# A two-layer step of matmul, mLSTM and sparse attention: layer 1 projects the unnormed x and scales the results; operand slices made during the tile before; page numbers read earlier

## The chip, the cores and the metric

The kernel runs on one core of one Trainium2 chip. The metric is device microseconds of one execution, from the first to the last instruction on that core with what the runtime adds around them. The engines are named as in the profile: PE (TensorE matmul), DVE (VectorE), ACT (ScalarE), POOL (GpSimd), SP (SyncE, which here only issues transfers and reads numbers into its registers).

## The reference, cut to what matters

A prompt of 512 tokens and 8 single-token decode samples (520 columns together) go through two layers of width 2048: a pool and mLSTM layer, then a sparse-attention layer with compressed, selected and window branches whose decode samples read a paged cache. Everything is float32.

```python
def rmsnorm(x, g):
    r = lax.rsqrt(jnp.mean(xf * xf, axis=-1, keepdims=True) + EPS)
    return (xf * r).astype(x.dtype) * g

def nsa_layer(x, ..., page_table, norm_g, w_in, b_gate, w_out):
    h = rmsnorm(x, norm_g)
    proj = jnp.einsum('btd,de->bte', h, w_in)
    q, kv_c, kv_s, kv_w, gts, z = split_cols(proj, (NSA_W, KV_W, KV_W, KV_W, 3 * N_HEADS, NSA_W))
    ...
    past_c = cache_kv_cmp[page_table].astype(f32)
    ...
    y = jnp.einsum('bte,ed->btd', o.reshape(B, T, NSA_W).astype(x.dtype) * jax.nn.silu(z), w_out)
    return x + y.astype(x.dtype), kv_c, kv_s, new_win
```

The first layer has the same frame: norm, input projection, mixing, a gate by silu(z), output projection, residual.

## The kernel before, in words

Activations lie transposed, features on the partitions: x is 16 slices of 128 features x 520 columns (`XY`). A projection is a **tile**: 128 output features, its weight 2048 x 128 (1 MB). The program has 146 tiles in a fixed order: one for the gates of layer 0, 16 for the pool part, 40 for the mLSTM (4 heads of 10), 16 for the output of layer 0 (`O0_BASE`), one for the gates of layer 1 (`G1_BASE`), 56 for the attention (`A_BASE`, 4 groups of 14), 16 for the output of layer 1 (`O1_BASE`).

Each float32 product is made of three reduced ones, so both operands are split in a high and a low part. The weight: SP loads `w_raw`, ACT writes its high part `w_hi` (`split_hi`), POOL subtracts and writes `w_lo` in four instructions (`split_lo`). There are two weight buffers: SP may load tile n+2 once POOL has split tile n; ACT splits tile n+2 after it has taken tile n out of PSUM. The activations: `h_hi` by ACT, `h_lo` by DVE, one slice of 16 at a time, made once for a whole stretch of tiles, since PE reads the same 16 slices for each tile. A tile is 96 matmuls (16 slices k, three products, two halves of 260 columns), and waits for the slices two at a time:

```python
for k in range(*part):
    ...
    if h_need is not None and k % 2 == 0:
        pe.wait_ge(S["h_ready"], h_need + k + 2)
```

The 16 slices are rewritten at four places. Before tile 0 and before tile `G1_BASE` they hold the normed x (`h_dve`, `h_act`: DVE multiplies by g and rstd into `x_res`, ACT copies to `h_hi`, DVE subtracts to `h_lo`). Before `O0_BASE` and `O1_BASE` they hold y, the mixed output (`y_split_act`, `y_split_dve`). At each place the rewriting starts when PE has done the last tile that reads the old slices, and PE waits for the first two.

What stands between the layers, in order: the 16 output tiles, during which DVE adds the residual (line 461) and the squares (line 464); the cross-partition sum on PE (`norm_pe`, line 404); rstd by DVE and ACT; the slices; tile `G1_BASE`; a sigmoid and seven small matmuls on the gates; then the first attention tile. In an output tile's turn ACT first squares the row that DVE has taken out (line 473), and only then splits the weight of the tile after next.

SP issues its transfers in one written order, and a wait in it holds all that follow. Before head 0 it issues the eight state loads (line 587), then the weight of the third mLSTM tile. After tile `G1_BASE`'s weights are on their way it saves x to DRAM (line 644) and reads the 32 page numbers into registers (`value_load`, line 650), from which the cache loads of line 670 get their addresses.

In the last part of each mLSTM head DVE updates the decode samples' state (line 1593, 16 instructions) before it normalises the head (lines 1596 to 1601). In an attention group ACT takes all 14 tiles out of PSUM: q, k, v rows with plain copies, the z tiles with a Silu (line 1356).

## Time and profile before

| what | value |
|---|---|
| median of three runs | 2301.4 us (2300.94 to 2303.07) |
| the profiled execution's own time | 2301.22 us |
| its span, first to last instruction | 2299.4 us |
| PE busy | 2165.9 us, 94% |
| DVE, ACT, POOL busy | 831.7, 735.6, 749.2 us |
| mean granted TensorE clock | 0.977 |

The profile lists busy time by engine, the waits between engines, and a timeline in microseconds from the span's start. Neighbouring instructions of one kind are merged in a timeline row, with their count behind an x. In square brackets stands how long the engine was idle before the row, and which instruction released it.

### The profile page before, as it was taken

The numbers are of one execution on the slowest core, as the hardware profiler recorded it, in microseconds if no ns is written. First come the engines' busy times: TensorE is split into PE (matmuls) and PEld (weight loads), VectorE is DVE, ScalarE is ACT, GpSimd is POOL, SyncE is SP. The second block draws the span as 40 slices with busy tenths as digits, with TensorE's granted clock in tenths as the row PEclk, the third lists the DMA queues.
The fourth block names the chain that finished last, engine by engine and source line by source line (L and its number), as shares of the span: only waits on it lengthen the run. The fifth ranks groups of instructions, "written<-read, shape, count | busy, mean of one in ns | idle before, by whom it ended". The sixth has DMA issues, their size and how long they took to land.

```text
span 2299.4 us, 44104 instructions
## 1 busy us (share of the span) xinstructions
PE 2165.9 (94%) x17957; PEld 2049.7 (89%) x17957; DVE 831.7 (36%) x1785; ACT 735.6 (32%) x1029; POOL 749.2 (33%) x588
## 2 busy tenths in 40 slices
PE   3899999999999989978999999999999999999996
PEld 3899999999999989977988998889888998889995
DVE  6412203333150361124246522652255423653114
ACT  4322123323232342223324332442334333343221
POOL 1244433433434234442330242124321233123440
PEclk7999999999999999989999999999999999999997
DMA  6223363746446354453544344343634344414431
GB/s 228 76 79 83 110 199 99 206 129 167 141 112 194 114 129 114 114 176 92 145 113 121 94 126 131 84 129 98 161 92 127 102 135 107 124 53 114 114 102 74
DMA packets 453106, 282.06 MB, mean 123 GB/s; under 512 B 17112, under 2 KB 445720, under 8 KB 450611
## 3 DMA queue, kind: packets, MB, share of 16 engines
q1 hardware_dynamic: 452939, 279.71, 43.5%
q8 instruction: 120, 1.97, 0.4%
q14 instruction: 47, 0.39, 0.1%
HBM read 250.86 MB, written 45.99 MB: 129 GB/s over the span
## 4 chain that ended last, share of the span: by engine, by line
PE 57%; issue 22%; POOL 10%; DVE 8%; ACT 2%; POOLq 0%; DVEq 0%; ACTq 0%
PE ps L365 45%; POOL w_lo L343 10%; PE ps L1028 2%; PE ps L1122 1%; PE ps L933 1%; PE ps L1062 1%; PE ps L1126 1%; PE ps L1100 1%; PE ps L958 1%; DVE scratch L1730 1%; PE ps L1130 1%; ACT scratch L1334 1%; DVE xy L1866 1%; DVE x_res L428 1%; DVE h_lo L425 0%
## 5 line engine op out<-in xcount | busy, mean ns | idle before, releaser
L343 POOL TENSOR_TENSOR w_lo<-w_raw,w_hi 128x512 fp32r<-128x512 f32 x584 | 749.0, 1314 | 1498.4 <-ACT w_hi L327 1167.6
L365 PE MATMUL ps<-h_hi,w_hi 128*128 128x260 f32 x4672 | 975.2, 290 | 58.0 <-DVE h_lo L425 35.4
L365 PE MATMUL ps<-h_hi,w_lo 128*128 128x260 f32 x4672 | 945.7, 284 | 0.0
L365 PE MATMUL ps<-h_lo,w_hi 128*128 128x260 f32 x4672 | 945.0, 284 | 0.0
L365 PEld LDWEIGHTS ps<-h_hi,w_hi 128*128 128x128 f32 x4672 | 728.4, 190 | 90.0 <-issue 62.1
L365 PEld LDWEIGHTS ps<-h_hi,w_lo 128*128 128x128 f32 x4672 | 725.0, 190 | 0.0
L365 PEld LDWEIGHTS ps<-h_lo,w_hi 128*128 128x128 f32 x4672 | 724.9, 190 | 0.0
L327 ACT ACTIVATE w_hi<-w_raw 128x2048 fp32r<-128x2048 f32 x134 | 256.8, 1916 | 27.0 <-DMA w_raw<-in_w_in 18.8
L461 DVE TENSOR_TENSOR xy<-ps,x_res 128x520 f32 x32 | 22.4, 700 | 282.0 <-PE ps L365 282.0
L473 ACT ACTIVATE scratch<-xy 128x520 f32 (+1 forms) x32 | 20.4, 639 | 281.3 <-DVE xy L461 281.3
L1334 ACT ACTIVATE scratch<-ps,scratch 128x128 f32<-128x128 f32 (+3 forms) x128 | 66.3, 523 | 134.1 <-DVE scratch L1758 133.6
L1716 DVE TENSOR_TENSOR scratch<-ps,scratch 128x520 f32<-128x520 f32 x24 | 16.8, 699 | 201.1 <-ACT rstd L1324 201.1
L1212 ACT ACTIVATE scratch<-ps 128x520 f32<-128x520 f32 x24 | 14.5, 604 | 209.2 <-PE ps L365 209.2
L1028 PE MATMUL ps<-scratch 128*128 128x128 f32 (+3 forms) x256 | 80.0, 435 | 0.0
L1509 DVE COPY scratch<-scratch 128x16 f32<-128x16 f32 x4 | 0.7, 184 | 169.7 <-ACT scratch L1212 169.7
L1346 ACT ACTIVATE scratch<-ps 128x128 f32<-128x128 f32 (+1 forms) x64 | 28.0, 437 | 100.0 <-PE ps L1100 99.6
L1028 PEld LDWEIGHTS ps<-scratch 128*128 128x128 f32 x256 | 41.1, 191 | 16.1 <-issue 11.0
L1322 ACT ACTIVATE scratch<-ps 128x520 f32<-128x520 f32 x16 | 9.7, 605 | 139.5 <-PE ps L365 139.5
L1641 DVE COPY scratch<-ps 128x512 f32<-128x512 f32 x32 | 22.1, 692 | 88.2 <-PE ps L933 87.7
L1757 DVE TENSOR_REDUCE scratch<-ps 128x2 f32<-128x256 f32 (+1 forms) x64 | 52.8, 825 | 2.2
L383 ACT ACT_TABLE_LOAD x39 | 50.0, 1283 | 0.9 <-ACT w_hi L327 0.2
L1122 PE MATMUL ps<-scratch 128*128 128x128 f32 x320 | 48.9, 284 | 0.0
(320 smaller groups left out, 1775.0 us busy)
## 6 DMA issues: line engine op xcount, KB each, us to landing
w_raw<-in_w_in SPq DMA_DIRECT2D x114, 1024.0 KB, 5.8
w_raw<-in_w_out SPq DMA_DIRECT2D x32, 1024.0 KB, 6.0
scratch<-in_cache_kv_sel SPq DMA_DIRECT2D x256, 64.0 KB, 1.9
scratch<-in_cache_kv_win SPq DMA_DIRECT2D x128, 128.0 KB, 2.5
scratch<-in_cache_kv_cmp SPq DMA_DIRECT2D x256, 64.0 KB, 2.0
out_kvw_s<-in_cache_kv_win SPq DMA_DIRECT2D x24, 512.0 KB, 6.7
x_scratch<-xy SPq DMA_DIRECT2D x2, 4160.0 KB, 14.3
x_res<-x_scratch SPq DMA_DIRECT2D x32, 260.0 KB, 6.0
```

The lines of the kernel that those rows point to most:

```text
L327: nc.scalar.activation(WH[:, t.p], WR[:, t.p], ACT.Copy).then_inc(S["w_hi"], 1); own.done("w_hi")
L343: ins = nc.gpsimd.tensor_tensor(WL[:, t.p, k:k + 4], WR[:, t.p, k:k + 4], WH[:, t.p, k:k + 4].bitcast(F32), ALU.subtract)
L365: mm = nc.tensor.matmul(PS[:, bank + c, 0:HALF], lhsT=w[:, t.p, k, :], rhs=h[:, k, c * HALF:(c + 1) * HALF], start=(k == 0 and x == 0), st ...
L383: own.step(nc.scalar.activation(CELL[:], ones[0:1, 0:1], func))
L428: nc.vector.scalar_tensor_tensor(XR[:, k % 2], XY[:, k], PR[:, gcol + k:gcol + k + 1], RS[:], ALU.mult, ALU.mult).then_inc(S["h_tmp"], 1); ...
L933: mm = T(PS[:, bank, pg * P:(pg + 1) * P], ring(u)[:, pg], ident)
L958: M(PS[at:at + 32, 6, 0:256], lhsT=zq[:, 32 * b:32 * b + 32], rhs=pt[:, kind, half * 256:(half + 1) * 256], start=(b == 0), stop=(b == NS ...
L1028: mm = M(PS[:, r, 0:(i + 1) * P], lhsT=qt[:, jj, i * P:(i + 1) * P], rhs=kT[:, r, 0:(i + 1) * P], start=True, stop=True)
L1122: M(PS[:, to, 0:P], lhsT=pt[:, 0, s * P:(s + 1) * P], rhs=vr[:, 0, s * P:(s + 1) * P], start=(s == 0), stop=(s == i))
L1334: ins = A(pr[:, 2 * (n % 2) + r, 0:L], PS[:, r, 0:L], ACT.Exp, bias=S1["st"][:, 4 + n % 2, r:r + 1], scale=SCALE, accum_out=S1["st"][:, n ...
L1346: A(pt[:, 0, 0:L], PS[:, 4, 0:L], ACT.Copy).then_inc(S["at_pta"], 1); own.done("at_pta")
L1757: step(V.tensor_reduce(st[:, 2 + n % 2], PS[:, 0:2, 0:(i + 1) * P], AX, ALU.max))
```

## The change

1. Layer 1 no longer norms x before it projects. The slices hold x times g, made by `xg_hi` (ACT) and `xg_lo` (DVE, one instruction with three inputs) slice by slice while PE still runs the last output tile of layer 0; a semaphore `k_read` tells which slices PE has read. rstd lies in a row `r1` of its own, and each result of layer 1 is multiplied by it when it leaves PSUM: the tiles of k and v rows, the z tiles and an extra instruction for q on DVE; cos and sin of the rotation are multiplied by it once. ACT keeps the Silu of z, now from SBUF, and drops its copies.
2. y is split slice by slice in the same way during the last tile before `O0_BASE` (slices 0 to 13) and during the last turns of group 3 before `O1_BASE` (slices 0 to 6).
3. In head 3 the 16 state updates stand behind all 16 slices; their eight stores stand in `out_sp` behind its third turn.
4. The page numbers get a buffer of their own, are loaded at the start and read into SP's registers behind the first state loads.
5. `norm_pe` and the small gate matmuls stand inside the tiles `G1_BASE` and `A_BASE`, behind slice 12.
6. One of the six stores of a group's rows is issued three tiles earlier, and the first eight cache units behind the second weight of group 0.

```diff
+                if tell and k < KT - 1:
+                    mm.then_inc(S["k_read"], 1)
...
-            own.step(nc.vector.reciprocal(RS[:], RS[:]))
-
-        def h_dve(dve, own, r, gcol):
+            own.step(nc.vector.reciprocal(RS[:] if out is None else out, RS[:]))
...
+        def xg_hi(act, own, k):
+
+            nc.scalar.activation(HH[:, k], XY[:, k], ACT.Copy, scale=PR[:, R_G1 + k:R_G1 + k + 1]
+                                 ).then_inc(S["h_hi"], 1); own.done("h_hi")
+
+        def xg_lo(dve, own, k):
+            dve.wait_ge(S["h_hi"], KT + k + 1)
+            nc.vector.scalar_tensor_tensor(HL[:, k], XY[:, k], PR[:, R_G1 + k:R_G1 + k + 1], HH[:, k].bitcast(F32),
+                                           ALU.mult, ALU.subtract).then_inc(S["h_ready"], 1); own.done("h_ready")
+
+        def y_hi(act, own, r, ks, done=None):
+
+            for k in ks:
+                if done is None:
+                    act.wait_ge(S["k_read"], (KT - 1) * (2 * r) + k + 1)
+                elif k == ks[0]:
+                    act.wait_ge(S["proj_done"], done)
                 nc.scalar.activation(HH[:, k], XY[:, k], ACT.Copy).then_inc(S["y_hi"], 1); own.done("y_hi")
...
+            empty(7, 0)
+            add_squares(7, 0)
+            for k in range(12 if r == 0 else 0):
+                xg_lo(dve, own, k)
+            empty(7, 1)
+            for k in range(12, 14 if r == 0 else 0):
+                xg_lo(dve, own, k)
+            add_squares(7, 1)
+            for k in range(14, KT if r == 0 else 0):
+                xg_lo(dve, own, k)
...
+            square(7, 0)
+            if r == 0:
+                split_hi(act, own, Tile(base, 0, 7, 2).ahead(2))
+                for k in range(14):
+                    act.wait_ge(S["k_read"], KT - 1 + k + 1)
+                    xg_hi(act, own, k)
+            square(7, 1)
+            if r == 0:
+                for k in range(14, KT):
+                    xg_hi(act, own, k)
+                split_hi(act, own, Tile(base, 1, 7, 2).ahead(2))
...
+            for i in range(8):
+                body(i, i == 7)
+                if i == 2 and late is not None:
+                    late()
...
+            sp.dma_start(PAGES[:], I["page_table"].rearrange("(o b) n -> o (b n)", o=1)).then_inc(S["small_in"], 16)
...
             load_states(0)
+            sp.wait_ge(S["small_in"], 16 * 10)
+            page_of = [sp.value_load(PAGES[0:1, x:x + 1], min_val=0, max_val=I["cache_kv_sel"].shape[0] - 1)
+                       for x in range(NS * NPG)]
...
-            out_sp(sp, 0, O0_BASE, G1_BASE)
+            out_sp(sp, 0, O0_BASE, G1_BASE, lambda: store_states(3))
...
+            project(pe, Tile(G1_BASE, 0), 2 * KT, part=(0, 12))
             norm_pe(pe, 1)
-            project(pe, Tile(G1_BASE, 0), 2 * KT)
-            pe.wait_ge(proj_read[1], (G1_BASE + 1) // 2)
+            project(pe, Tile(G1_BASE, 0), 2 * KT, part=(12, KT))
...
+                    project(pe, Tile(A_BASE, 0, g, 14), part=(0, 12))
+                    gates()
+                    project(pe, Tile(A_BASE, 0, g, 14), part=(12, KT))
...
+                if h == 3:
+                    act.wait_ge(S["m_yz"], 8)
+                    act.wait_ge(S["pl_y"], 9)
+                    y_hi(act, own, 0, range(KT - 2))
...
-                        if r < 4:
-                            A(halves(qr[:, r]), ps2(t), ACT.Copy)
...
+                        z = XR[:, (n // 4) % 2]
+                        A(z, z, ACT.Silu).then_inc(S["a_z"], 1); own.done("a_z")
...
+                    if g == 3 and n >= 12:
+                        y_hi(act, own, 1, ((), range(0, 4), range(4, 7), ())[n - 12])
...
+                if h < 3:
+                    new_states()
...
+                if h == 3:
+                    y_lo(dve, own, 0, range(KT - 2))
...
+                if h == 3:
+                    y_lo(dve, own, 0, range(KT - 2, KT))
+                    new_states()
...
+            TT(cosT, cosT, r1, ALU.mult)
+            step(TT(sinT, sinT, r1, ALU.mult))
...
+                        TT(halves(XR[:, (0, 1, None, 0, None, 1)[x]]), ps2(t), halves(r1), ALU.mult
+                           ).then_inc(proj_read[t.p], 1)
...
+                        if r < 4:
+                            TT(halves(qr[:, r]), ps2(t), halves(r1), ALU.mult)
...
+                            TT(halves(XR[:, jj % 2]), PS[:, 2:4, 0:HALF], halves(r1), ALU.mult).then_inc(proj_read[t.p], 1)
...
+                        y_lo(dve, own, 1, ((), (), range(0, 4), range(4, 7))[n - 12])
```

SP's queue at the start of head 0, before. L587 are the state loads, L303 the weight loads of the third mLSTM tile and on, L598 copies of the window cache:

```order
L587 DMA scratch<-in_state_mlstm_c 128x2x256 x8
L303 DMA w_raw<-in_w_in 128x16x128 [waits w_split]
L598 DMA out_kvw_s<-in_cache_kv_win 16x8192
L303 DMA w_raw<-in_w_in 128x16x128 [waits w_split]
L598 DMA out_kvw_s<-in_cache_kv_win 16x8192
```

The same place in the changed kernel, where L675 is the read of one page number (32 of them) and L304 the weight load:

```order
L625 DMA scratch<-gate_scratch 128x1048 x3
L630 DMA scratch<-in_state_mlstm_c 128x2x256 x8
L675 TENSOR_LOAD pages [waits small_in]
L675 ISA x2
L675 TENSOR_LOAD pages
...
L675 ISA x2
L304 DMA w_raw<-in_w_in 128x16x128 [waits w_split]
L647 DMA out_kvw_s<-in_cache_kv_win 16x8192
L304 DMA w_raw<-in_w_in 128x16x128 [waits w_split]
```

The 32 reads now stand between the state loads and the third tile's weight.

DVE at the end of head 3, before. L1593 is the state update, L1596 to L1608 the norm and gate of the head, L450 the low parts, L461 the first output tile's results:

```order
L1588 TENSOR_TENSOR scratch<-scratch 128x520 [waits m_sq,m_nev]
L1593 SCALAR_TENSOR_TENSOR scratch<-scratch 128x256 [waits v_in,c_sc,m_sqs]
L1593 SCALAR_TENSOR_TENSOR scratch<-scratch 128x256 [waits m_cn] x15
L1596 TENSOR_SCALAR rstd<-ps 128x520 [waits m_ssq,m_cn]
L1598 RECIPROCAL rstd<-rstd 128x520 [waits m_sqrt,m_var]
L1601 SCALAR_TENSOR_TENSOR xy<-xy,params,rstd 128x520 [waits dve_step]
L1601 SCALAR_TENSOR_TENSOR xy<-xy,params,rstd 128x520
L1608 TENSOR_TENSOR xy<-xy,scratch 128x520 [waits proj_read0,dve_step]
L1608 TENSOR_TENSOR xy<-xy,scratch 128x520 [waits m_yz]
L450 TENSOR_TENSOR h_lo<-xy,h_hi 128x520 [waits m_yz,n_out,y_hi,st_out]
L450 TENSOR_TENSOR h_lo<-xy,h_hi 128x520 [waits y_hi,h_ready] x15
L455 MEMSET rstd 128x520 [waits h_ready]
```

And in the changed kernel (L1647 the state update, L464 the low parts, L1666 the gate):

```order
L1652 TENSOR_SCALAR rstd<-ps 128x520 [waits m_ssq,m_sqs]
L1654 RECIPROCAL rstd<-rstd 128x520 [waits m_sqrt,m_var]
L1657 SCALAR_TENSOR_TENSOR xy<-xy,params,rstd 128x520 [waits dve_step]
L1657 SCALAR_TENSOR_TENSOR xy<-xy,params,rstd 128x520
L464 TENSOR_TENSOR h_lo<-xy,h_hi 128x520 [waits y_hi,dve_step]
L464 TENSOR_TENSOR h_lo<-xy,h_hi 128x520 [waits y_hi,h_ready] x13
L1666 TENSOR_TENSOR xy<-xy,scratch 128x520 [waits proj_read0,h_ready]
L1666 TENSOR_TENSOR xy<-xy,scratch 128x520 [waits m_yz]
L464 TENSOR_TENSOR h_lo<-xy,h_hi 128x520 [waits y_hi,m_yz]
L1647 SCALAR_TENSOR_TENSOR scratch<-scratch 128x256 [waits v_in,c_sc,h_ready]
L1647 SCALAR_TENSOR_TENSOR scratch<-scratch 128x256 [waits m_cn] x15
L480 MEMSET rstd 128x520 [waits n_out,st_out,m_cn]
```

The low parts moved ahead of the gate, and the 16 state updates moved from before the norm to just ahead of the output tiles.

ACT from the last output tile of layer 0 on, in the changed kernel (L501 squares, L328 the split of a weight, L444 the slices of x times g, L399 the square root for rstd). Before, the 16 slices stood behind the square root:

```order
L501 ACTIVATE scratch<-xy 128x520 [waits sq_sum,proj_read1]
L328 ACTIVATE w_hi<-w_raw 128x2048 [waits proj_done,w_loaded1,sq_made]
L444 ACTIVATE h_hi<-xy,params 128x520 [waits k_read,w_hi]
L444 ACTIVATE h_hi<-xy,params 128x520 [waits k_read,h_hi] x13
L501 ACTIVATE scratch<-xy 128x520 [waits sq_sum,proj_read0,h_hi]
L444 ACTIVATE h_hi<-xy,params 128x520 [waits sq_made]
L444 ACTIVATE h_hi<-xy,params 128x520 [waits h_hi]
L328 ACTIVATE w_hi<-w_raw 128x2048 [waits proj_done,w_loaded0,h_hi]
L386 ACT_TABLE_LOAD [waits proj_read1,proj_read0]
```

The split of the first attention tile's weight (the second L328) now stands behind all 16 slices.

## Rows read from the trace of the kernel before

**Rows 1.** The page, part 1: engine, busy us, share, instructions.

```profile
PE 2165.9 (94%) x17957; PEld 2049.7 (89%) x17957; DVE 831.7 (36%) x1785; ACT 735.6 (32%) x1029; POOL 749.2 (33%) x588
```

**Rows 2.** Waits of PE by releaser: us in total, times, longest.

```profile
PE ps L365 <- DVE h_lo L425: 35.4, 14, 12.0
...
PE ps L365 <- ACT x_res L1356: 4.2, 12, 0.7
```

**Rows 3.** Timeline of PE: start us, us, what [idle before, releaser].

```profile
306.26 0.80 PE L365 MATMUL ps<-h_hi,w_hi 128*128 128x260 f32 x2 [3.41 <-POOL w_lo L343]
...
831.52 0.77 PE L365 MATMUL ps<-h_hi,w_hi 128*128 128x260 f32 x2 [6.37 <-DVE h_lo L450]
...
1032.04 0.77 PE L365 MATMUL ps<-h_hi,w_hi 128*128 128x260 f32 x2 [10.05 <-DVE h_lo L425]
...
2067.36 0.33 PE L1051 MATMUL ps<-c_common,scratch 128*128 128x128 f32 x1 [1.67 <-DVE scratch L1776]
...
2074.60 0.77 PE L365 MATMUL ps<-h_hi,w_hi 128*128 128x260 f32 x2 [6.91 <-DVE h_lo L450]
```

**Rows 4.** Timeline of SP, ACT and POOL at the first mLSTM tiles.

```profile
289.62 0.63 SPq L303 DMA_DIRECT2D w_raw<-in_w_in  x1
...
299.26 1.92 ACT L327 ACTIVATE w_hi<-w_raw 128x2048 fp32r<-128x2048 f32 x1 [7.21 <-DMA w_raw<-in_w_in]
...
301.25 4.96 POOL L343 TENSOR_TENSOR w_lo<-w_raw,w_hi 128x512 fp32r<-128x512 f32 x4 [19.60 <-ACT w_hi L327]
...
320.91 0.60 ACT L1212 ACTIVATE scratch<-ps 128x520 f32<-128x520 f32 x1 [14.63 <-PE ps L365]
```

**Rows 5.** DMA issues: count, KB each, median us to landing.

```profile
w_raw<-in_w_in SPq DMA_DIRECT2D x114, 1024.0 KB, 5.8
...
scratch<-in_state_mlstm_c SPq DMA_DIRECT2D x8, 256.0 KB, 8.4
...
x_scratch<-xy SPq DMA_DIRECT2D x1, 4160.0 KB, 12.0
```

**Rows 6.** Line 650 alone, two stretches: ns min/median/max, first and last start us.

```profile
L650 SPq TENSOR_LOAD <-scratch x10: 395/860/877, 1019.6 to 1029.6; - x10
...
L650 SPq TENSOR_LOAD <-scratch x23: 263/266/395, 1029.6 to 1042.2; - x23
```

**Rows 7.** Timeline of DVE, ACT and POOL, head 3 to the output tiles.

```profile
822.37 1.43 DVE L1601 SCALAR_TENSOR_TENSOR xy<-xy,params,rstd 128x520 f32<-128x520 f32 x2
...
845.60 0.70 DVE L461 TENSOR_TENSOR xy<-ps,x_res 128x520 f32 x1 [1.35 <-PE ps L365]
...
857.00 0.70 DVE L461 TENSOR_TENSOR xy<-ps,x_res 128x520 f32 x1 [9.12 <-PE ps L365]
...
820.14 0.20 ACT L383 ACTIVATE act_cell<-c_common 1x1 f32<-1x1 f32 x1
...
827.82 10.68 ACT L445 ACTIVATE h_hi<-xy 128x520 fp32r<-128x520 f32 x16
...
827.87 6.35 POOL L343 TENSOR_TENSOR w_lo<-w_raw,w_hi 128x512 fp32r<-128x512 f32 x4 [6.02 <-ACT w_hi L327]
849.33 5.02 POOL L343 TENSOR_TENSOR w_lo<-w_raw,w_hi 128x512 fp32r<-128x512 f32 x4 [15.12 <-ACT w_hi L327]
```

**Rows 8.** Single lines of DVE: ns min/median/max, first and last start.

```profile
L450 DVE TENSOR_TENSOR h_lo<-xy,h_hi x32: 699/700/1671, 828.6 to 2084.0; 128x520 fp32r<-128x520 f32 x32
...
L1593 DVE SCALAR_TENSOR_TENSOR scratch<-scratch x64: 483/485/1398, 402.4 to 816.5; 128x256 f32<-128x256 f32 x64
...
L428 DVE SCALAR_TENSOR_TENSOR x_res<-xy,params,rstd x9: 759/761/1852, 40.9 to 55.3; 128x520 f32<-128x520 f32 x9
```

**Rows 9.** Timeline of DVE and ACT around the tile of the gates.

```profile
1018.46 0.70 DVE L461 TENSOR_TENSOR xy<-ps,x_res 128x520 f32 x1 [9.15 <-PE ps L365]
...
1072.97 0.60 ACT L1322 ACTIVATE scratch<-ps 128x520 f32<-128x520 f32 x1 [14.65 <-PE ps L365]
```

**Rows 10.** Timeline of DVE at the start of the last output tiles.

```profile
2089.26 0.70 DVE L461 TENSOR_TENSOR xy<-ps,x_res 128x520 f32 x1 [3.86 <-PE ps L365]
```

255 lines of the change are left out of this document (130 added, 125 removed).

## The prediction, made blind

> **What bounds the kernel now.** The page's first part comes first: PE is busy 94% of the span [rows 1], so time can only come out of the gaps of PE or out of stretches in which its clock is low. The waits of PE by releaser say who makes the gaps: the low parts that DVE writes for slices of x (35.4 us) are the largest, and ACT's Silu of the z tiles costs 4.2 us in twelve short waits [rows 2]. The timeline of PE says where: 3.41 us ahead of the third mLSTM tile, for a weight; 6.37 us ahead of the output tiles of layer 0; 10.05 us and more at the tile of the gates; 1.67 and 6.91 us ahead of the last output tiles [rows 3]. The first 48 us are not touched by the change, except for one small load more.
>
> A bare tile takes 11.4 us: two successive output tiles are taken out at 845.60 and 857.00 [rows 7]. With it each place has a price, low clock included. From PE's stop at 831.52 - 6.37 = 825.15 to 845.60 are 20.4 us for one tile: 9 us lost. From the last output tile (1018.46) to the first attention tile (1072.97) are 54.5 us [rows 9] for two tiles (22.9) and about 1.8 us for the square sum and the small matmuls: 29.8 us lost. From 2067.4 [rows 3] to 2089.26 [rows 10] are 21.9 us for one tile: 10 us lost. If all of this went and nothing came, 53 us would be gained with the 4.2. I go through the places, because at each one something is put in the way.
>
> **Term 1, page numbers: +16.6.** In front of the third mLSTM tile PE already waits 3.41 us, and the chain behind it is SP's queue: the weight is issued at 289.62, split by ACT from 299.26 (1.92 us), by POOL from 301.25 (4.96 us), and PE starts at 306.26 [rows 3, 4]. The change puts the 32 reads into this queue, ahead of this weight. In the old place they took from 1019.6 to about 1042.7, where they held nothing that PE waited for. The single line shows two speeds: the first ones come 1.11 us apart, the last 22 intervals take 12.6 us, 0.57 us each [rows 6]. The slow ones lie under the save of x, 4.2 MB that land in 12 us [rows 5]. In the new place the state loads are in flight: the last is issued some 2 us before 289.6 and lands 8.4 us later [rows 5], so about four reads are slow and 28 fast: 4.4 + 16.0 = 20.4 us. Then the weight is issued at 310.0, lands 5.8 us later [rows 5] (not 9.6, the state loads are through), ACT 2.0, POOL 5.0: PE starts at 322.9, not 306.26. That is 16.6 us, all on the path: PE has nothing else to do from 302.9 on. All fast would give +14.5, all slow 35.5 us of reads and +31.7. The gap has low clock behind it: the tile begun at 306.26 is taken out at 320.91 [rows 4], 14.65 us where 11.4 and 0.3 would do, so 2.9 us; that is paid before the change too. The next weights are queued behind in the same rhythm and have a tile's time each. In layer 1 nothing is won back, because the cache units that stood behind the reads are needed four tiles later.
>
> **Term 2, the page table's load at the start: +0.4**, one issue more ahead of the small loads; bounds 0 and 1.
>
> **Term 3, output tiles of layer 0: +4.4.** ACT can begin the high parts when its table is in, at 820.4, and needs 10.68/16 = 0.67 us for one [rows 7]; DVE begins the low parts at 823.8, behind the norm, and needs 0.73 us (0.70 [rows 8] and a gap). So PE finds slices 0 and 1 ready at 825.3 and runs on at its own 0.72 us a slice. Two things follow. First, ACT does 14 slices before it takes out the last head tile and splits the next weight: 14 x 0.67 from 820.4, then 0.6 and 1.9 us, end at 832.3, where the split was through at 827.8; POOL's four instructions start at 832.4. While POOL runs, DVE's instruction with both inputs in SBUF does not take 0.70 but up to 1.67 us [rows 8], and POOL's four take 6.35 instead of 5.02 us [rows 7]. The low parts 12 and 13 and the two gate products fall into that: the gate is ready at 839.3, slices 14 and 15 at 840.8 and 841.6. PE waits about 2 us ahead of slice 12 and 4 us ahead of slice 14; the first output tile ends at 843.1, 2 us earlier than before. Second, the 16 state updates now stand ahead of the output tiles: 16 x 0.52 = 8.3 us [rows 8], the zeroing of the row 0.9, so DVE takes the first output tile out at 850.9, not 845.6. Behind that stand ACT's square, the split of the third output tile's weight and POOL: this took from 845.6 to 854.35 [rows 7], 8.8 us. So the third tile can start at 859.7, where it started at 856.7: a loss of 3 us, whatever PE won before it. PE idles 2.5 to 5 us there, and I add 1.4 for a phase of low clock. Bounds: -6 (the updates hide) and +7.
>
> The Trainium skill (SBUF — State Buffer, "Who interferes with whom") says that a VectorE instruction with two SBUF inputs contends with a GpSimd instruction that reads SBUF. The rows agree: 0.70 against 1.67 us. A sum without that rule would have the gate ready 4 us earlier here, and terms 4 and 5 better by 3 us and 2 us.
>
> **Term 4, the gates' tile: -23.5.** Seen from the last output tile's end at 1018.3: ACT squares the row before, splits the weight of the gates' tile until 1010.7, and then makes 14 high parts at 0.67 us, until 1020.1; DVE's instruction of three inputs takes 0.79 us a slice, but up to 1.85 us beside POOL [rows 8], which is busy until 1017.4. So it has slice 3 at 1018.0 and slice 11 at 1024.3, and PE, which needs them from 1018.3 on at 0.72 us, is not held. DVE then takes the last output tile out (1024.3 to 1025.1, 6 us later than before), ACT squares it, makes slices 14 and 15 and only then splits the first attention tile's weight: 1027.2 to 1029.1; POOL until 1034.2. PE is through with the gates' tile and the square sum at 1031.1: it waits 3.2 us, for a weight. Then the first attention tile with its seven small matmuls, 12.7 us, ends at 1047. Before, it ended at 1072.5. That is 25.4 us; a gap of 3.2 us is like that of 3.41 at 306, so I take two thirds of its 2.9 us of low clock off. Bounds: -29 (the weight in time) and -20 (low clock, and the split held up further). The reciprocal and the scaling of cos and sin lie under the first attention tile.
>
> **Term 5, last output tiles: -6.** Low parts 0 to 3 stand in turn 14 ahead of an addition that PE's next transposes wait for; four of them are 2.9 us, of which I count 1.2 as free: PE starts 1.7 us later. The three in turn 15 delay the last combination by 0.75 more. PE then starts the output tile at 2070.2 instead of 2074.6, reaches slice 6 at 2074.5, and waits 1 us for slice 7, because the last gate product runs beside POOL (1.67 us by rows 8) and the low parts follow at 0.73 us. The tile ends at 2082.9, not 2088.9. Bounds -9 and -2.
>
> **Term 6, inside the groups: -3.** DVE gets 4 x 12 multiplications of 0.70 us = 34 us, ACT loses 32 instructions of 0.60. Where DVE's multiplication replaces ACT's copy (k, v, z), the next step on DVE begins as early as before; q's stands behind ACT's swap, which comes 0.6 us sooner. The z banks come free at once, so the 4.2 us of rows 2 go. I take 3 of them. Bounds: -4.2, and +8 if a quarter of the new work lies on the path.
>
> **Sum.** 16.6 + 0.4 + 4.4 - 23.5 - 6 - 3 = -11.1. The profiled execution took 2301.2 us (span 2299.4), the median is 2301.4; the forecast is 2290.
>
> **The rivals.** (a) The gain comes nearly whole: the state updates hide, the weight is in time, POOL disturbs less (-5, -29, -9, -4 with +16): about 2270. For it speaks that PE's gaps are large; against it the order of ACT. 17%. (b) The new DVE work lies on the path in the groups: +8 in term 6 instead of -3, 2301, no change. PE and DVE work there in short turns that hand over to each other; against it, ACT drops nearly as much work as DVE gets, in the same turns. 10%. (c) Slower: the page reads stay at 1.1 us each, which costs 15.1 us more, 2305. It decides from 0.9 us a read on. Against it: SP issues nothing while it reads, so the traffic ends by itself. 7%. (d) The forecast, 2280 to 2297: 58%. The remaining 8% is spread on both sides.
>
> **How the numbers follow.** A measurement of this kernel tells 0.2% (4.6 us) from no change. Faster by more: (a), nine tenths of (d), some of the rest: 0.78. Within 0.2%: (b) and the upper end of (d): 0.13. Slower: (c) and a part of the rest: 0.09. The range 2268 to 2301 leaves out the worst of (c) and the best of (a). The likeliest case's own range is 2280 to 2297.
>
> **What would show each step.** Term 1: PE idle 19 to 21 us ahead of the third mLSTM tile, the weight issued near 310. Term 3: two waits of PE inside the first output tile, one for a weight ahead of the third, POOL's split for it starting near 854. Term 4: about 3 us for a weight ahead of the first attention tile, and no wait for slices. Term 5: one wait of 1.7 us in turn 15 and one of 1 us in the output tile. Term 6: the wait on the z tiles gone. The prediction is wrong if the reads take other than 18 to 24 us, if the low parts are not slowed beside POOL, or if the multiplications hold up a turn.

## The result and the profile after

The changed kernel takes 2286.4 us (median of six runs, 2283.6 to 2292.6), the kernel before 2300.5 us beside it (2299.6 to 2303.1): the ratio is 0.9939, with a 95% interval of 0.9926 to 0.9953. That is 14 us less, where 11 were forecast. The profiled execution of the changed kernel is the quickest of its six, 2283.63 us with a span of 2281.9 us, so the two profiles lie 17.5 us apart. The accounts by place below are made from the profiles, against 17.5, and so they come out some 3 us better than the medians.

Page, part 1, of the changed kernel, to lay beside [rows 1]:

```profile
PE 2152.8 (94%) x17957; PEld 2042.5 (90%) x17957; DVE 874.5 (38%) x1820; ACT 718.6 (31%) x998; POOL 757.6 (33%) x588
```

DVE works 43 us more and ACT 17 us less, and the kernel is still faster: neither is the bound. PE is busy 13 us less for the same 17957 matmuls, mostly because less of its time has the low clock (the mean granted clock is 0.981, before 0.977). The waits of PE by releaser (us in total, times, longest), against [rows 2]:

```profile
PE ps L366 <- POOL w_lo L344: 25.1, 3, 18.0
PE ps L366 <- DVE h_lo L428: 19.3, 7, 12.0
...
PE ps L366 <- DVE h_lo L464: 5.9, 3, 3.9
...
PE ps L1095 <- DVE scratch L1865: 4.0, 4, 1.0
```

The 35.4 us for the normed slices have become 19.3 (what is left is the start of layer 0), and the 4.2 us behind ACT's Silu are gone. In their place stand 25.1 us for weights (before 3.4), 18.0 of them in one wait. The last row is small but new in its size: before, the same wait was 1.6 us (term 6 comes back to it). The timeline of PE (start, us, what, in square brackets the idle time before and its releaser) says where, against [rows 3]:

```profile
319.87 0.80 PE L366 MATMUL ps<-h_hi,w_hi 128*128 128x260 f32 x2 [18.03 <-POOL w_lo L344]
...
848.44 0.51 PE L366 MATMUL ps<-h_hi,w_hi 128*128 128x260 f32 x2 [1.67 <-DVE h_lo L464]
...
854.07 0.80 PE L366 MATMUL ps<-h_hi,w_hi 128*128 128x260 f32 x2 [3.92 <-DVE h_lo L464]
...
872.85 0.77 PE L366 MATMUL ps<-h_hi,w_hi 128*128 128x260 f32 x2 [4.24 <-POOL w_lo L344]
...
1051.92 0.80 PE L366 MATMUL ps<-h_hi,w_hi 128*128 128x260 f32 x2 [2.86 <-POOL w_lo L344]
...
2052.23 1.06 PE L1159 MATMUL ps<-c_common,scratch 128*128 128x128 f32 x8 [1.70 <-DVE scratch L1917]
...
2059.76 0.33 PE L1110 MATMUL ps<-c_common,scratch 128*128 128x128 f32 x1 [2.69 <-DVE scratch L1845]
```

An account by place comes from the starts of the tiles, counted off in PE's rows (96 matmuls a tile). Each line is the start of a tile in us, before and after; what the difference gains or loses from one line to the next happened in between.

| tile | before | after | difference |
|---|---|---|---|
| first of the mLSTM | 279.52 | 278.52 | -1.0 |
| fourth of the mLSTM | 320.65 | 333.58 | +12.9 |
| first of head 3 | 690.04 | 702.79 | +12.8 |
| fourth output tile, layer 0 | 868.23 | 886.54 | +18.3 |
| second of the attention | 1072.41 | 1065.81 | -6.6 |
| first of group 3 | 1814.37 | 1804.76 | -9.6 |
| second output tile, layer 1 | 2088.85 | 2071.97 | -16.9 |
| end of the span | 2299.4 | 2281.9 | -17.5 |

So the page reads cost 13.9 us (term 1, forecast 16.6), the output tiles of layer 0 5.6 (term 3, forecast 4.4), the tile of the gates gives 24.9 (term 4, forecast 23.5), each group gives 1.0 (term 6, 4.0 in all, forecast 3), and the last output tiles give 7.3 less the group's 1.0, so 6.3 (term 5, forecast 6). The beginning, the heads and the end make up the other 1.8.

How firm these numbers are, the profiles of the experiments below show, where the code of a place is the same. Where the reads stand as here, the mLSTM's first three tiles take 55.0 to 55.5 us in all eight. The gates' tile and the first attention tile take 29.3 to 29.5 us, but once 30.7; the first three groups 738.9 to 739.1, but once 737.9. Two places spread more, and the granted clock with them: from the first to the fourth output tile of layer 0 it is 48.7 us here and 47.8 to 49.3 in seven others, so term 3 is 4.6 to 6.1. And the first output tile of layer 1 takes 11.8 us here, at a granted clock of 1.00, but 12.9 to 13.1 in seven of eight others, at 0.87 to 0.89. The one other kernel with the old code there (experiment 3) takes 1.2 us less, from the first tile of group 3, than the kernel before. So term 5 lies between -3.6 and -6.3, and 1.3 of the 3 us by which the profiles differ more than the medians are found here.

The largest gain, at the tile of the gates, was not undone in a run, and the changes 5 and 6 were not tried alone. What the rows of the kernel before show is PE's waits from 1018 to 1073 us:

```profile
PE ps L365 <- DVE h_lo L425: 17.0, 7, 10.1
PE ps L404 <- DVE rstd L464: 2.5, 1, 2.5
PE ps L901 <- ACT x_res L1266: 2.1, 1, 2.1
PE ps L365 <- DVE scratch L1631: 1.0, 1, 1.0
```

These are 22.6 us. In the changed kernel one wait of 2.86 us is left of them, and the mean granted clock there is 0.99 in the gates' tile and 0.89 in the next, where it was 0.81 over the whole stretch.

### The profile page after: what moved, and what is told of

Same layout as the page of the kernel before. It is cut to its first block, busy times and chain, and to the rows that moved or that the text cites. A ratio compares the mean times of both kernels' runs of the same rounds, so it can differ in the third digit from the quotient of the medians.

```text
span 2281.9 us, 43898 instructions
## 1 busy us (share of the span) xinstructions
PE 2152.8 (94%) x17957; PEld 2042.5 (90%) x17957; DVE 874.5 (38%) x1820; ACT 718.6 (31%) x998; POOL 757.6 (33%) x588
## 3 DMA queue, kind: packets, MB, share of 16 engines
q8 instruction: 123, 2.02, 0.4%
## 4 chain that ended last, share of the span: by engine, by line
PE 45%; issue 32%; POOL 15%; DVE 6%; ACT 1%; POOLq 0%; DVEq 0%; ACTq 0%
PE ps L366 33%; POOL w_lo L344 15%; PE ps L1087 3%; PE ps L1182 2%; PE ps L1159 2%; PE ps L1186 1%; PE ps L986 1%; PE ps L1121 1%; PE ps L1011 1%; DVE scratch L1799 1%; PE ps L1190 1%; DVE scratch L1788 1%; DVE xy L1944 1%; DVE scratch L1790 0%; PE ps L997 0%
## 5 line engine op out<-in xcount | busy, mean ns | idle before, releaser
L344 POOL TENSOR_TENSOR w_lo<-w_raw,w_hi 128x512 fp32r<-128x512 f32 x584 | 757.4, 1328 | 1473.1 <-ACT w_hi L328 1144.3
L366 PE MATMUL ps<-h_hi,w_hi 128*128 128x260 f32 x4672 | 973.4, 290 | 50.4 <-POOL w_lo L344 25.1
L328 ACT ACTIVATE w_hi<-w_raw 128x2048 fp32r<-128x2048 f32 x134 | 256.7, 1916 | 120.2 <-PE ps L366 79.8
L473 DVE TENSOR_TENSOR xy<-ps,x_res 128x520 f32 (+1 forms) x32 | 22.4, 700 | 269.1 <-PE ps L366 268.7
L501 ACT ACTIVATE scratch<-xy 128x520 f32 (+1 forms) x32 | 20.4, 639 | 278.9 <-DVE xy L473 278.9
L1375 ACT ACTIVATE rstd<-ps 64x520 f32<-64x520 f32 x24 | 14.4, 602 | 210.4 <-PE ps L366 210.4
L1272 ACT ACTIVATE scratch<-ps 128x520 f32<-128x520 f32 x24 | 14.5, 605 | 208.4 <-PE ps L366 208.4
L1784 DVE TENSOR_TENSOR scratch<-ps,scratch 128x520 f32<-128x520 f32 x16 | 11.2, 700 | 113.8 <-ACT rstd L1376 113.8
L1159 PE MATMUL ps<-c_common,scratch 128*128 128x128 f32 x320 | 45.8, 274 | 3.5 <-DVE scratch L1881 1.8
```

The lines of the kernel that those rows point to most:

```text
L328: nc.scalar.activation(WH[:, t.p], WR[:, t.p], ACT.Copy).then_inc(S["w_hi"], 1); own.done("w_hi")
L344: ins = nc.gpsimd.tensor_tensor(WL[:, t.p, k:k + 4], WR[:, t.p, k:k + 4], WH[:, t.p, k:k + 4].bitcast(F32), ALU.subtract)
L366: mm = nc.tensor.matmul(PS[:, bank + c, 0:HALF], lhsT=w[:, t.p, k, :], rhs=h[:, k, c * HALF:(c + 1) * HALF], start=(k == 0 and x == 0), st ...
L1159: mm = T(PS[:, 4 + r, s * P:(s + 1) * P], pr[:, 2 * (n % 2) + r, s * P:(s + 1) * P], ident)
```

## The experiments

Twelve kernels, four at a time (1 to 4, then 5 to 8, then 9 to 12), each four beside the kernel before on the same chip: 2299.0, 2300.9 and 2301.4 us. By its ratio of 0.9939 the changed kernel stands at 2284.9, 2286.8 and 2287.4 us there; "less" and "more" below are against these. Each ratio has an interval of about 0.0013 to either side, some 3 us.

### 1 to 3: the page reads

Back in their old place:

```diff
-            load_states(0)
-            sp.wait_ge(S["small_in"], 16 * 10)
-            page_of = [sp.value_load(PAGES[0:1, x:x + 1], ...
...
             sp.wait_ge(S["consts"], 16 * 4)
+            sp.wait_ge(S["small_in"], 16 * 10)
+            page_of = [sp.value_load(PAGES[0:1, x:x + 1], ...
```

> The changed kernel with the 32 page number reads put back to their old place in SP's queue, behind the save of x in layer 1; the page table keeps its own buffer and its early load. My theory (term 1: the reads cost their own length ahead of the third mLSTM tile, and nothing else): PE waits about 3.4 us there instead of 18.0, so 13.9 us go. But in layer 1 the save of x is now issued only when the last output tile is taken out (1042.6 us in the changed kernel), so 23 us of reads end 14 us after the first attention tile began, and the weight of the third attention tile is issued late: it would land 5.8 us after the reads, ACT 1.9, POOL 5.0, and PE waits about 2 us for it. Net 2274 us. Rival 1 (the reads are hidden in layer 1 altogether, as in the kernel before): 2272, no wait at the third attention tile. Rival 2 (the wait ahead of the third mLSTM tile is the state loads' traffic, not the reads): the wait stays at 18 us and the time at 2286 or above.

In four lots, during the output tiles of layer 0:

```diff
+            def late(i):
+                if i == 2:
+                    store_states(3)
+                if 3 <= i <= 6:
+                    read_pages(8)
+            out_sp(sp, 0, O0_BASE, G1_BASE, late)
```

> The changed kernel with the 32 reads in four lots of eight, behind turns 3 to 6 of SP's queue in the output tiles of layer 0. Eight reads take 8 x 0.55 = 4.4 us; a turn of two tiles has 23 us, of which SP uses about 4. My theory: no tile waits for a weight there, and the whole cost of term 1 goes: 14 us less than the changed kernel, about 2272. Rival (the reads slow the queue so that residual slices or weights come late): one wait of 1 to 4 us in each of the four turns, 2276 to 2288.

And the kernel before with this move alone:

```diff
             load_states(0)
+            sp.wait_ge(S["small_in"], 16 * 10)
+            page_of = [sp.value_load(PAGES[0:1, x:x + 1], ...
```

> The kernel before with the page reads alone moved to where the changed kernel has them (own buffer, table loaded at the start). My theory: PE waits 17 to 18 us ahead of the third mLSTM tile instead of 3.4, and nothing is given back in layer 1: 2301 + 14 = 2315 us. Rival (in the kernel before the reads delayed cache units or weights in layer 1, and moving them is part of the gain there): the attention part is shorter by 2 us or more, and the total is below 2313.

Measured: 2275.8 us (ratio 0.9900, 0.9885 to 0.9915), 2272.7 us (0.9883, 0.9868 to 0.9899), and 2314.3 us (1.0065 to the kernel before, 1.0051 to 1.0078). All three are as the theory had them. The traffic rival is out, since the wait goes with the reads and comes with them.

The chain in the changed kernel, from the reads on. First all 32 reads in one row (shortest, median and longest in ns, then the first and the last start in us), then the timelines of SP, ACT and POOL:

```profile
L675 SPq TENSOR_LOAD <-pages x32: 265/267/481, 288.8 to 306.6; - x32
```

```profile
307.17 0.38 SPq L304 DMA_DIRECT2D w_raw<-in_w_in  x1
...
312.90 1.91 ACT L328 ACTIVATE w_hi<-w_raw 128x2048 fp32r<-128x2048 f32 x1 [21.87 <-DMA w_raw<-in_w_in]
...
314.88 9.95 POOL L344 TENSOR_TENSOR w_lo<-w_raw,w_hi 128x512 fp32r<-128x512 f32 x8 [34.23 <-ACT w_hi L328]
```

Read it as the prediction did: 32 reads from 288.8 to 307.1, 5.7 us to landing, 1.9, 5.0, and PE at 319.87.

In the old place the reads are not free in the new kernel. They begin when x is saved, and the weight behind them goes out late; the rows are SP's reads, SP's next weight, and PE at the third attention tile:

```profile
L691 SPq TENSOR_LOAD <-pages x32: 261/268/914, 1030.8 to 1053.7; - x32
```

```profile
1054.20 1.98 SPq L304 DMA_DIRECT2D w_raw<-in_w_in  x2
...
1067.08 0.51 PE L366 MATMUL ps<-h_hi,w_hi 128*128 128x260 f32 x2 [1.65 <-POOL w_lo L344]
```

In the kernel before, 42 us lay between the last read (1042.2, [rows 6]) and this tile (1083.9); here it is 13. So the move is worth 1.8 us between the starts of the second and the third attention tile, and it was paid for with 13.9. In four lots the reads cost nothing that the profile shows: no wait in the output tiles that the changed kernel doesn't have, the thirteen tiles from the fourth on take 149.9 us in both, and there is no wait at the third attention tile.

### 4: the state updates of head 3 back ahead of the norm

```diff
-                if h < 3:
-                    new_states()
+                new_states()
...
                     y_lo(dve, own, 0, range(KT - 2, KT))
-                    new_states()
```

> The changed kernel with the 16 state updates of head 3 back ahead of the norm, as in the heads before; their stores stay where the change put them. In the changed kernel DVE stands idle for 6.9 us ahead of the norm's variance and ACT takes the square root only at 830.6 us, so the updates cost nothing there. My theory (term 3: the updates push the first take-out to 863.5, behind it the weight of the third output tile, for which PE waits 4.2 us and then has a phase of low clock): the wait goes, and the low clock behind it (6.8 us at half speed): 6 to 7 us less, 2280. Rival 1 (the low parts start later because the updates hold up the norm, beside POOL): PE's waits inside the first output tile grow by as much as the other goes, 2284 to 2287. Rival 2 (the third tile's weight is late for another reason, POOL beside the low parts): the wait of 4.2 us stays, 2286.

Measured: 2280.7 us, ratio 0.9928 (0.9915 to 0.9942), 4 us less. By the tile starts it is 5.4 us, from the first output tile to the fourth (43.4 us), and 4.4 to 5.9 against the spread of the kernels that have the old order. The waits of PE there in the changed kernel are the three rows above (1.67, 3.92, 4.24); in this one the third is gone and the others stand:

```profile
848.02 0.51 PE L366 MATMUL ps<-h_hi,w_hi 128*128 128x260 f32 x2 [1.66 <-DVE h_lo L464]
853.65 0.80 PE L366 MATMUL ps<-h_hi,w_hi 128*128 128x260 f32 x2 [3.93 <-DVE h_lo L464]
```

So the late weight of the third output tile hung on the updates alone, and ahead of the norm they are free. Both rivals are out by these rows. The times alone don't show it: 4 us between two ratios with such intervals is just short of clear.

### 5 and 6: the first attention tile's weight, by DVE's order and by ACT's

```diff
-            for k in range(12 if r == 0 else 0):
+            for k in range(10 if r == 0 else 0):
                 xg_lo(dve, own, k)
             empty(7, 1)
-            for k in range(12, 14 if r == 0 else 0):
+            for k in range(10, 14 if r == 0 else 0):
```

> The changed kernel with one instruction of DVE moved: it takes the last output tile of layer 0 out of PSUM behind the tenth low part of x times g instead of the twelfth, so before its tile of the gates is two slices old. In the changed kernel it did so at 1041.92 us, ACT stood idle for 3.5 us for it, squared the row, made slices 14 and 15 and split the first attention tile's weight only at 1044.9; PE waited 2.86 us for POOL behind it. My theory (term 4: the wait is made by the order, not by the load of the weight): the split begins near 1041.4, POOL is through at 1048.4, the wait is gone: 3 to 4 us less than the changed kernel with its low clock, 2282. Rival (the weight's load is the limit: it is issued at 1034.98 and lands some 5.8 us later): the split can't begin before 1041 and the wait shrinks by less than 1 us.

```diff
             if r == 0:
+                split_hi(act, own, Tile(base, 1, 7, 2).ahead(2))
+            square(7, 1)
+            if r == 0:
                 for k in range(14, KT):
                     xg_hi(act, own, k)
-                split_hi(act, own, Tile(base, 1, 7, 2).ahead(2))
```

> The changed kernel with ACT's split of the first attention tile's weight ahead of the square of the last row and of slices 14 and 15, instead of behind them. It can begin when the weight has landed, near 1041, so 4 us sooner, and POOL begins near 1043. Theory A (DVE's instructions with two inputs in SBUF are slowed while POOL runs): POOL now lies over the addition of squares, the first take-out's end and low parts 14 and 15, which go from 0.70 to up to 1.7 us each; PE waits 0.5 to 1 us for the square sum and 1 us for slices 14 and 15 inside the tile of the gates, and what the weight wait loses (2.86 us) is mostly given back: 1 to 2 us less than the changed kernel, 2285. Theory B (no slowing): nothing waits, 3 to 4 us less, 2282.

Measured: 2286.8 us (0.9938, 0.9924 to 0.9951), no less than the changed kernel, and 2284.6 us (0.9924, 0.9910 to 0.9938), 2 us less. In the first my theory missed: a wait stays. The rival's number came (the wait is 0.96 us shorter, less than 1), but not for its reason. The take-out, the split, POOL and PE in it:

```profile
1039.44 0.70 DVE L473 TENSOR_TENSOR xy<-ps,x_res 128x520 f32<-128x520 f32 x1
...
1042.42 1.92 ACT L328 ACTIVATE w_hi<-w_raw 128x2048 fp32r<-128x2048 f32 x1
...
1044.09 2.46 DVE L449 SCALAR_TENSOR_TENSOR h_lo<-xy,params,h_hi 128x520 fp32r<-128x520 f32 x2
...
1044.42 5.73 POOL L344 TENSOR_TENSOR w_lo<-w_raw,w_hi 128x512 fp32r<-128x512 f32 x4 [10.34 <-ACT w_hi L328]
...
1050.20 0.51 PE L366 MATMUL ps<-h_hi,w_hi 128*128 128x260 f32 x2 [1.90 <-POOL w_lo L344]
```

DVE reaches the take-out 3.9 us after the tile has ended, because it is that far behind with the low parts; the split begins 6.9 us after the gates' tile has begun, where it was 8.4, and the wait is 1 us shorter. The weight's load (it had landed by 1039.7) is not the limit. In the second, with the split ahead of the square, POOL starts 4.7 us into the gates' tile (8.9 in the first, 10.4 in the changed kernel) and lies over DVE's addition of squares:

```profile
1042.58 6.93 POOL L344 TENSOR_TENSOR w_lo<-w_raw,w_hi 128x512 fp32r<-128x512 f32 x4 [6.22 <-ACT w_hi L328]
...
1046.75 1.64 DVE L478 TENSOR_TENSOR rstd<-rstd,scratch 128x520 f32<-128x520 f32 x1
...
1048.45 1.14 PE L407 MATMUL ps<-rstd,c_common 128*128 128x260 f32 x4 [1.76 <-DVE rstd L478]
```

The weight is in time and PE waits 1.76 us for the square sum instead: the addition took 1.64 us beside POOL, where it takes 0.70 without. This is theory A ("no slowing" would leave no wait), though the wait is all at the sum and none at the slices. From the start of the gates' tile to that of the second attention tile the changed kernel takes 29.3 us, this one 27.0.

### 7: each multiplication by rstd twice

```diff
+                        step(TT(halves(XR[:, (0, 1, None, 0, None, 1)[x]]), ps2(t), halves(r1), ALU.mult))
                         TT(halves(XR[:, (0, 1, None, 0, None, 1)[x]]), ps2(t), halves(r1), ALU.mult
```

and in the same way for q and z.

> The changed kernel in which each of DVE's 48 multiplications by rstd in the attention groups (k and v rows, q, z) is made twice, the second over the first with a wait between: 48 x 0.73 = 35 us of DVE work more; nothing else. My theory (term 6: these lie beside other work, so they cost nothing): less than 4 us in all four groups, no more than 1 us a group, 2286 to 2290. Rival (b) of the prediction (a part of DVE's work lies on the path of PE): a quarter would be 9 us, all of it 35 us, 2295 to 2321.

Measured: 2304.5 us, ratio 1.0018 (1.0009 to 1.0028), 18 us more; the two profiles lie 15.4 us apart. My theory fell. Twelve more multiplications in a group (8.8 us) cost 3.8 us in group 0 and 2.6 and 2.7 us in the next two. The tile starts of group 0 say which: nothing for the four q tiles, 1.7, 1.0 and 1.0 us in the three tiles behind, where the first rows of k and v are taken out, nothing at the z tiles. The waits of PE that grew, in the changed kernel and then in this one:

```profile
PE ps L974 <- DVE scratch L1708: 3.3, 4, 0.8
...
PE ps L1011 <- DVE scratch L1703: 0.7, 4, 0.2
```

```profile
PE ps L974 <- DVE scratch L1708: 10.1, 12, 0.9
PE ps L1011 <- DVE scratch L1703: 7.4, 4, 1.8
```

L974 are PE's transposes of the rows, L1011 its matmuls with cached keys, whose copies by DVE queue behind: there the second multiplication is on the path, at q and z it is not. The three groups make 9.1 us; another 4.4 lie in group 3 and 2.4 in the first of the last output tiles, and these were not taken apart. Note what this test shows: what one more multiplication would cost, not what the first one did.

### 8 and 9: the early slices of y in the last group

A group's attention scores are worked in 16 turns, and turns 14 and 15 are the last. All 16 slices made behind the group (the early calls removed, `range(7, ...)` back to `range(0, ...)`):

> The changed kernel without the early slices of y for layer 1's output: all 16 high and low parts are made behind the last group, as before the change. My theory (term 5): PE's waits of 1.70 and 2.69 us in the last turns go, but a wait of about 7 us for the first low parts comes back ahead of the last output tiles, with its low clock: 6 us more than the changed kernel, 2292 to 2293. Rival (the early slices only move DVE's work, and the last slices come at the same time either way): 0 to 2 us more, 2287.

And only DVE's low parts in another order:

```diff
                         TT(on[:, 2], on[:, 2], PS[:, 4, 384:416], ALU.add).then_inc(S["d_vs"], 1); own.done("d_vs")
+                        if g == 3:
+                            y_lo(dve, own, 1, range(0, 4))
...
                     combine(n)
+                if g == 3:
+                    y_lo(dve, own, 1, range(4, 7))
                 backed(15)
```

> The changed kernel with the early low parts of the last group in another order: low parts 0 to 3 behind the small addition for which PE waited 1.70 us in turn 14, and 4 to 6 behind the last combination, for which PE waited 2.69 us. My theory (both waits are of no consequence, since DVE works without a pause from there to low part 15, and the last output tiles' first can't end before it): the two waits shrink, PE starts the output tile 1 to 4 us sooner and waits inside it instead, and its end, the time, is the same within 1 us: 2286. Rival (the waits are on the path, as term 5 priced them): 1.7 us or more less, 2282 to 2284.

Measured: 2292.4 us (0.9965, 0.9952 to 0.9978), 6 us more, as forecast. By the tile starts, from the first tile of group 3 to the second output tile, it is 5.6 us against the changed kernel's own profile and 4.1 to 4.5 against the seven with the lower clock in that tile. And 2289.3 us (0.9944, 0.9931 to 0.9958), which the times can't tell from the changed kernel. In its profile the wait of 1.70 us is gone, with one of 0.43 behind it, and that of 2.69 is 2.02, so PE begins the output tile 1.8 us sooner. Then it waits inside it:

```profile
2062.67 5.21 DVE L464 TENSOR_TENSOR h_lo<-xy,h_hi 128x520 fp32r<-128x520 f32 x3
...
2070.68 0.50 PE L366 MATMUL ps<-h_hi,w_hi 128*128 128x260 f32 x2 [1.51 <-DVE h_lo L464]
```

These three low parts took 2.17 us in the changed kernel, before POOL began, and 5.21 here beside it, so the last low part ends 1.3 us later. The second output tile starts 268.6 us after the first tile of group 3: 267.2 in the changed kernel's profile, but 268.2 to 268.6 in the seven others with its order. So nothing was won, as my theory had it. The waits of 1.70 and 2.69 us are not what holds the end: DVE's work is, up to the last low part, and the order decides only whether POOL lengthens some of it.

### 10 to 12: the gate sooner, and the versions put together

```diff
-                    y_hi(act, own, 0, range(KT - 2))
+                    y_hi(act, own, 0, range(7))
                 act.wait_ge(S["proj_done"], t.n + 1)
                 A(halves(S0["kT"][:, 1]), ps2(t), ACT.Silu)...
+                if h == 3:
+                    y_hi(act, own, 0, range(7, KT - 2))
+                    act.wait_ge(S["m_yz"], 10)
+                    y_hi(act, own, 0, range(KT - 2, KT), O0_BASE)
                 split_hi(act, own, t.ahead(2))
...
-                    y_lo(dve, own, 0, range(KT - 2))
+                    y_lo(dve, own, 0, range(4))
```

In these texts z_early is experiment 10, "the fourth experiment" is 4 above, and experiments 11 and 12 are the versions put together.

> The kernel with the state updates back ahead of the norm (the fourth experiment), and one thing more: in head 3 ACT takes the last z tile out behind seven high parts of y instead of fourteen, and splits the next weight only behind all sixteen; DVE makes the two gate products behind low part 3 instead of 13. In the changed kernel the two products ran beside POOL, 1.67 us each, and PE waited 3.9 us for slices 14 and 15 behind them. My theory (the wait is made by the order of the gate and by POOL beside it): the products now run before POOL starts and take 0.70 us; PE waits some 2 us at slice 4 or 6 for the products, and 2 to 3 us at the last slices, because POOL still lies over the last low parts: 1 to 3 us less than the 2280.7 of the fourth experiment, 2278. Rival (DVE's work and the 5 us of POOL beside it are the limit, whatever the order): no change, 2281, with the waits at other slices.

> The changed kernel with three things: the page reads in four lots of eight during the output tiles, the state updates ahead of the norm, and DVE's take-out of the last output tile behind low part 5 of x times g (the fifth experiment had it behind 9, where DVE reached it 3.9 us after PE had ended the tile). Each mends one place and they don't touch one another, so they should add: 13 us for the reads, 3 to 5 for the updates, 2 to 3 for the take-out with no wait left ahead of the first attention tile: 2265 to 2268. Rival (the take-out's place gives nothing as in the fifth experiment, because POOL then lies over low parts 12 to 15): a wait of over 1 us stays and the time is 2268 to 2270.

> The same three things and the earlier gate of z_early. If z_early gives 1 to 3 us, this is 2263 to 2266; if the limit there is DVE's work beside POOL, it is as the run before.

Measured: 2279.0 us (0.9905, 0.9890 to 0.9920), 2266.4 us (0.9854, 0.9841 to 0.9868) and 2263.2 us (0.9831, 0.9814 to 0.9847). The second and third also have `range(6)` and `range(6, 14)` in the place of the 10 of experiment 5, and the reads of experiment 2. The last is 24 us less than the changed kernel and 38 less than the kernel before. In experiment 12, PE's waits in the first output tile and in the tile of the gates are:

```profile
830.73 0.51 PE L366 MATMUL ps<-h_hi,w_hi 128*128 128x260 f32 x2 [1.19 <-DVE h_lo L464]
838.53 0.51 PE L366 MATMUL ps<-h_hi,w_hi 128*128 128x260 f32 x2 [1.66 <-DVE h_lo L464]
841.91 0.51 PE L366 MATMUL ps<-h_hi,w_hi 128*128 128x260 f32 x2 [1.67 <-DVE h_lo L464]
...
1026.95 1.15 PE L407 MATMUL ps<-rstd,c_common 128*128 128x260 f32 x4 [1.67 <-DVE rstd L478]
1030.33 0.51 PE L366 MATMUL ps<-h_hi,w_hi 128*128 128x260 f32 x2 [0.80 <-DVE h_lo L449]
```

From the first output tile to the fourth the kernel with the updates back (experiment 4) takes 43.4 us, with the earlier gate (experiment 10) 40.1; the three tiles after the fourth take 34.6. The intervals of these two overlap (0.9928 and 0.9905), but the profile has the gain: two waits, 5.6 us together, have become three, 4.5 us together (1.19 ahead of slice 4, 1.66 and 1.67 ahead of 12 and 14), and the mean granted clock in the tile is 1.00, where it was 0.89. Experiment 12 against 11 repeats it, with 2.3 us by the tile starts.

The last two rows, which experiment 11 has too, are the rival of experiment 11. With the take-out at low part 5 the weight is in time, but POOL then lies over the square sum and the last low parts, and PE waits 1.67 and 0.80 us for these instead of 2.86 for the weight. The place gives 1.5 us by the tile starts (27.9 us from the gates' tile to the second attention tile, where it was 29.3), not 2 to 3. Nearly all of that is clock: in the first attention tile it is 1.00 behind these shorter waits, where it was 0.89 behind the longer one. So the mechanism was the rival's, though the time lies in my range; 3 us of interval don't tell the two apart.

## Why the prediction was right, point by point

**The forecast** (2290, own range 2280 to 2297) was the case that happened; the median is 3.6 us lower. The order of the terms was right, and each lies within its own bounds but the first, which is 0.6 us under its lower one. Two things in it don't hold by its own numbers. The chances of the three outcomes don't follow from those of the cases: faster by more can be at most 0.77 by its parts (0.17 + 0.52 + 0.08), and no change is at least 0.16. And in rival (b) "ACT drops nearly as much work as DVE gets" is 32 x 0.60 = 19 against 34 us; the pages have 17 against 43.

**Term 1, page numbers.** The chain and the absence of cover were right. Mis-sized was "about four reads are slow": none was, and 32 reads took 18.3 us instead of 20.4. Counted from the first mLSTM tile, PE starts the third one 14.6 us later, the bound for all fast, and some low clock that the kernel before paid behind its own wait makes it 13.9 at the fourth. The state loads were in flight as I had put it; from their rows, in the changed kernel:

```profile
L630 SPq DMA_DIRECT2D scratch<-in_state_mlstm_c x8: 486/695/2276, 280.6 to 286.5; - x8
...
DMA to landing us min/median/max: 7.9/8.4/8.8
```

So the last one landed between 294.4 and 295.3, when nine or ten reads had run beside the loads, and none but the first took over 0.28 us (the first takes 0.48 to 0.50 in every profile with the reads here or in lots). What failed is the step from the save of x to the state loads: that a read beside any traffic is slow. Rival (c), 1.1 us a read, needs what stands below under the hardware. And "in layer 1 nothing is won back" holds for the kernel before (in experiment 3 the third attention tile starts 11.5 us after the second, as without the move) but not for the changed one, where it is worth 1.8 us.

**Term 2, the table's load.** Not resolved: the first tile of all starts at 47.8 us before and 48.4 after, but in the other kernels with this load it starts anywhere from 47.5 to 48.5.

**Term 3, output tiles of layer 0.** Both waits in the first tile stood where they were put (ahead of slices 12 and 14; about 2 and 4 us forecast, 1.67 and 3.92 measured), for the reason given: the gate products beside POOL. DVE, from the low parts on, and POOL under it:

```profile
839.90 8.49 DVE L464 TENSOR_TENSOR h_lo<-xy,h_hi 128x520 fp32r<-128x520 f32 x9
848.42 3.34 DVE L1666 TENSOR_TENSOR xy<-xy,scratch 128x520 f32<-128x520 f32 x2
...
854.05 8.30 DVE L1647 SCALAR_TENSOR_TENSOR scratch<-scratch 128x256 f32<-128x256 f32 x16
...
863.47 0.70 DVE L473 TENSOR_TENSOR xy<-ps,x_res 128x520 f32 x1 [0.45 <-DVE rstd L480]
...
844.80 6.41 POOL L344 TENSOR_TENSOR w_lo<-w_raw,w_hi 128x512 fp32r<-128x512 f32 x4 [10.65 <-ACT w_hi L328]
```

The updates push the take-out, the take-out the weight, and PE waits 4.24 us (2.5 to 5 forecast). With the 12.8 us of the places before taken off, the third tile starts 3.4 us later than before (3 forecast). The rest of the miss is the low clock behind the wait, from the profile's windows (us, busy PE, PEld, DVE, ACT, POOL, then the granted clock):

```profile
873.00:887.00 14.00, 14.00 (x100) 14.00 (x101) 0.05 (x1) 0.00 (x0) 4.63 (x4) 0.84 0.68 188
```

A clock of 0.84 over 14 us is 2.2 us, where 1.4 was allowed; in the seven other profiles with this code the wait is 2.4 to 4.3 us.

The Trainium skill's rule that was weighed here (SBUF — State Buffer, "Who interferes with whom": a VectorE instruction with two SBUF inputs contends with a GpSimd instruction that reads SBUF) agrees with the rows above: 0.70 us without POOL against 1.67 beside it. The same profile shows the limits of it. An addition of that size with one input in PSUM took 0.70 us beside POOL (L473, at 868.76). But a copy of only 128x8 from SBUF, with one input, took 1.15 us beside POOL (at 1194.09) and 0.17 without it (at 1258.98), and the sum had no price for such copies.

**Term 4, the gates' tile.** -24.9 for -23.5. "About 3 us for a weight ahead of the first attention tile, and no wait for slices" was 2.86 us and no wait. The order was as told: DVE took the last output tile out 5.4 us after PE had ended it (6.0 forecast), and ACT stood idle for it. In the changed kernel POOL's 5 us for this weight come behind DVE's last low part, and PE waits for POOL itself. In experiments 5, 6, 11 and 12 POOL comes earlier and lies over DVE's last instructions, and PE still waits 1.8 to 2.5 us, for POOL or for DVE. The gain of the term as a whole rests on the rows and on the sum, not on a run that undoes it.

**Term 5, last output tiles.** -6.3 for -6, or down to -3.6 by other profiles of the same code, and 4 to 6 when undone: the size was right within that. One of its steps was not: the wait of 1.7 us in turn 15 came as forecast (1.70), but the wait for slice 7 inside the output tile did not come; it stood ahead of the tile, as 2.69 us at the last combination, where I had counted 0.75. Experiment 9 shows that the two are the same DVE time seen at two places.

**Term 6, inside the groups.** -1.0 a group for -0.75. The Silu wait went as told, with 4.2 us. But rival (b) had more in it than the text gave it, though its +8 us did not happen. One multiplication is plainly on the path in the changed kernel: that of the last row stands on DVE ahead of a copy that PE waits for (L1865). Before, the copy's wait was

```profile
PE ps L1036 <- DVE scratch L1795: 1.6, 4, 0.4
```

and now it is 4.0 us (L1095, shown above), 0.6 us more in each group. What holds it up is this row, 0.70 us long:

```profile
1193.35 0.70 DVE L1765 TENSOR_TENSOR x_res<-ps,scratch 128x520 f32<-128x520 f32 x1
```

At the other rows of k and v the new waiting is 0.2 us a group (L1011 in experiment 7). That it is so little may be because the multiplication replaced a copy by ACT of nearly the same length (0.60 and 0.70 us); no run shows it. Doubled, the multiplications cost 2.6 to 3.8 us a group.

## What to carry to other kernels

A queue that is only "in the background" is on the path where a consumer already waits for it: 18 us of register reads cost 14 of them ahead of a weight that was late anyway, and nothing when cut into lots of 4.4 us behind weights that had 23 us a turn. Moving work off a visible wait pays as long as some engine has the room; here the room on DVE ran out beside POOL, and reordering after that mostly moved the wait, for 1.5 to 3 us a place, a good part of it clock. To learn whether there is room for one more instruction, double it: a third of the added time came out on the path, at places where the profile had shown 0.2 us of new waiting a group. To learn what the first one costs, lay the waits of before and after side by side: that showed 0.6 us a group. And when one profile is laid against another, look at several profiles of the same code first: here one tile took 11.8 us at a granted clock of 1.00 and 13.1 at 0.87, in kernels with the same code.
